# Subtracting the low part of the edge weight unit on GpSimd instead of VectorE in a two-layer DiT kernel

## The reference

```
h = h + 0.5 * mod_l[:, 2] * swiglu(pre_norm(h, norm_g[i, 0], mod_l, 0), ffn_w_in[i, 0], ffn_w_out[i, 0])
hn = pre_norm(h, norm_g[i, 1], mod_l, 1)
h = h + mod_l[:, 5] * y_l
h = h + 0.5 * mod_l[:, 8] * swiglu(pre_norm(h, norm_g[i, 2], mod_l, 2), ffn_w_in[i, 1], ffn_w_out[i, 1])
```

## Time and profile before

| what | us |
|---|---|
| median of 3 runs (lowest, highest) | 3191.51 (3191.02, 3193.46) |
| the profiled execution | 3189.59 |
| its span | 3187.9 |
| PE busy | 3075.0 (96%) |
| DVE busy | 1820.9 (57%) |
| ACT busy | 864.7 (27%) |
| POOL busy | 36.7 (1%) |
| granted TensorE clock, mean | 0.989 |

### The profile page before, as it was taken

How to read it: one execution, slowest core, us unless ns; L and a number is a source line. 1 busy time by engine, 2 the same in 40 slices (tenths; PEclk the granted TensorE clock), 3 DMA queues, 4 the chain that set the end, 5 groups by cost and what they waited for, 6 DMA issues and landing times.

```text
span 3187.9 us, 42477 instructions
## 1 busy us (share of the span) xinstructions
PE 3075.0 (96%) x17592; PEld 2638.7 (83%) x17592; DVE 1820.9 (57%) x2652; ACT 864.7 (27%) x1188; POOL 36.7 (1%) x73
## 2 busy tenths in 40 slices
PE   6999999999999899999999999999899999999999
PEld 4888888877777788888888888888788888888887
DVE  4675565864565576655565365656654546454444
ACT  3211121343443431111223111112322223242221
POOL 0000000000000000000000000000000000000000
PEclk8999999999999999999999999999899999999999
DMA  6332322111010043323221132322111212122222
GB/s 241 133 132 99 112 105 92 53 47 53 27 53 27 30 156 119 119 93 118 105 92 54 66 110 97 112 106 87 53 48 59 79 39 79 40 80 94 97 94 84
DMA packets 40984, 277.81 MB, mean 87 GB/s; under 512 B 4352, under 2 KB 5632, under 8 KB 8000
## 3 DMA queue, kind: packets, MB, share of 16 engines
q1 hardware_dynamic: 31024, 205.85, 17.8%
q0 software_dynamic: 9872, 70.72, 6.2%
HBM read 274.45 MB, written 2.10 MB: 87 GB/s over the span
## 4 chain that ended last, share of the span: by engine, by line
PE 90%; DVE 6%; ACT 2%; issue 1%; DMA 0%; SPq 0%; DVEq 0%; ACTq 0%
PE ps L305 29%; PE ps L306 28%; PE ps L307 28%; PE ps L625 2%; PE ps L333 1%; DVE wl L1273 1%; ACT wh L891 1%; DVE act_buf L1357 1%; DVE xnl L1361 1%; PE ps L319 0%; DMA ada_w<-ada 0%; PE ps L351 0%; ACT xnh L922 0%; DVE nrm L1570 0%; PE ps L418 0%
## 5 line engine op out<-in xcount | busy, mean ns | idle before, releaser
L305 PE MATMUL ps<-xnh,wl 128*128 128x512 f32 (+1 forms) x3040 | 1062.5, 350 | 31.4 <-DVE wl L1273 15.6
L306 PE MATMUL ps<-xnl,wh 128*128 128x512 f32 (+1 forms) x3040 | 1052.3, 346 | 0.0
L307 PE MATMUL ps<-xnh,wh 128*128 128x512 f32 (+1 forms) x3040 | 1051.7, 346 | 0.0
L305 PEld LDWEIGHTS ps<-xnh,wl 128*128 128x128 f32 x3040 | 580.7, 191 | 113.7 <-DVE wl L1273 17.5
L307 PEld LDWEIGHTS ps<-xnh,wh 128*128 128x128 f32 x3040 | 580.9, 191 | 70.8
L306 PEld LDWEIGHTS ps<-xnl,wh 128*128 128x128 f32 x3040 | 581.2, 191 | 68.2 <-issue 1.0
L1273 DVE TENSOR_TENSOR wl<-raw,wh 128x2048 fp32r<-128x2048 f32 (+1 forms) x183 | 410.3, 2242 | 145.3 <-ACT wh L891 145.1
L891 ACT ACTIVATE wh<-raw 128x2048 fp32r<-128x2048 f32 (+1 forms) x178 | 332.7, 1871 | 578.8 <-PE ps L307 578.8
L1415 DVE SCALAR_TENSOR_TENSOR h<-ps,coef,h 128x512 f32<-128x512 f32 x624 | 371.7, 642 | 116.1 <-PE ps L307 115.5
L305 PE MATMUL ps<-hidh,wl 128*128 128x512 f32 (+1 forms) x1232 | 425.0, 345 | 3.1 <-DVE h L1373 3.1
L306 PE MATMUL ps<-hidl,wh 128*128 128x512 f32 (+1 forms) x1232 | 426.0, 346 | 0.0
(11 more groups left out here) (233 smaller groups left out, 3056.9 us busy)
## 6 DMA issues: line engine op xcount, KB each, us to landing
raw<-weights SPq DMA_DIRECT2D x183, 1024.0 KB, 4.8
adaw<-ada POOLq DMA_DIRECT2D x64, 1024.0 KB, 5.0
ada_w<-ada SPq DMA_DIRECT2D x8, 1024.0 KB, 20.0
h<-x_in SPq DMA_DIRECT2D x1, 2048.0 KB, 8.6
c_act<-c_rows POOLq DMA_DIRECT2D x2, 1024.0 KB, 5.1
out<-h SPq DMA_DIRECT2D x8, 256.0 KB, 2.0
h<-x_in SPq DMA_DIRECT2D x1, 1024.0 KB, 28.9
cs<-rope_mla POOLq DMA_DIRECT2D x1, 512.0 KB, 3.5
```

Of the source, the lines that this page charges most:

```text
L305: mm(dst, lhs[1][rows], rhs[0][rows], start=first, stop=False)
L306: mm(dst, lhs[0][rows], rhs[1][rows], start=False, stop=False)
L307: return mm(dst, lhs[0][rows], rhs[0][rows], start=False, stop=last)
```

## The change

The semaphore `edge_hi` is new. ScalarE's last quarter of the edge unit counts it in place of `w_hi[s]`, and `split_lo(s)` goes from VectorE's `last_y`. GpSimd has a new `edge_lo(s)`, which waits for `edge_hi` and does the same subtraction, 128 x 2048, and counts `w_ready[s]`. It is called five times in GpSimd's list: behind the first `ada_loop`, behind the `cs` DMA, behind the 24th unit of the second round (whose loop is cut in two there), and twice at the end.

```diff
+            def edge_lo(s):
+                pool.wait_ge(edge_hi, c.next(edge_hi))
+                nc.gpsimd.tensor_tensor(wl[:, s, :], raw[:, s, :], wh[:, s, :].bitcast(F32), ALU.subtract).then_inc(w_ready[s], 1)
...
             c.next(ada_used, 2)
+            edge_lo(0)
             c.next(xn_ready, 2 * KD)
             pool.wait_ge(xn_ready, c.next(xn_ready, 2 * KD))
             pool.dma_start(cs[:], rope_mla).then_inc(tab_full, 16)
+            edge_lo(1)
             pool.wait_ge(xn_ready, c.next(xn_ready, 2 * KD))
             ada_start(mid)
-            ada_loop(mid + 2, (ADA_UNITS - ADA_0 - mid - 2) // 2)
+            end = ADA_2 - ADA_0
+            ada_loop(mid + 2, (end - mid) // 2)
+            edge_lo(0)
+            ada_loop(end + 2, (ADA_UNITS - ADA_0 - end - 2) // 2)
             pool.wait_ge(ada_used, c.next(ada_used, 2))
             pool.dma_start(cr[:], rope_ret).then_inc(tab_full, 16)
             pool.dma_start(dist[:], dist_in).then_inc(tab_full, 16)
+            edge_lo(1)
+            edge_lo(1)
...
                 if q == 3:
-                    ins.then_inc(w_hi[s], 1)
+                    ins.then_inc(edge_hi, 1)
...
                 add_pair(2 if early is not None else 4, parts[1], banks)
-                split_lo(s)
                 for m in (4, 6) if early is not None else (6,):
```

More of the change, by code:

```diff
@@ L196, in build @@
         ada_full = [sem(f"ada_full{s}") for s in range(2)]
+        edge_hi = sem("edge_hi")
         ada_used, ada_evac = sem("ada_used"), sem("ada_evac")
```

## The result

The changed kernel takes 3212.11 us (median of 4 runs, 3206.92 to 3215.10), the kernel before 3191.9 in the same comparison: a ratio of 1.0062, 95% interval 1.0046 to 1.0077. The forecast was 3211.0. The profiled execution took 3209.45 us with a span of 3207.7, 19.8 more than before.

What follows compares the result with a forecast made beforehand. TensorE, busy for 3075.0 of 3187.9 us, was taken to bound the kernel; 13.1 us of later second chains plus 6.4 of lost clock made 19.5 us slower, a median of 3211.0 us, range 3188 to 3215.

Steps and rivals of the forecast that it cites:

- What can be gained: TensorE's waits for the moved unit at edges 1, 3, 4 and 5: 4.5 us, 0.14% of the time.
- How long GpSimd takes: GpSimd's 128 x 2048 subtraction at each edge: 4.6 us, twice VectorE's time.
- The collision: At the edges, GpSimd's reading may meet VectorE's two-input L1361 rows; taken to delay the second chains by 13.1 us in all.
- The priced end: Each L1361 that falls into GpSimd's 4.6 us waits for its end: 13.1 us over five edges; forecast's chance 0.50.
- the other end: GpSimd and VectorE read beside each other at full pace, no price: sum -2.7 us, 3188.8; chance 0.26.
- Which row: At edge 1 GpSimd gets in behind row 5's low part at 614.60; row 6's low part waits until 619.20.
- The clock: TensorE falls to 1.2 GHz behind the long stalls: 1.6 us at each of edges 1 to 4, 6.4 us.
- By edge: Second chain later by 2.85 us at edges 1, 3 and 4, 2.6 at edge 2, 1.95 at edge 5, before clock loss.
- Shared in turns: GpSimd and VectorE both slowed while overlapping at the edges, none blocked to the end: about +1 us, 3192.5; chance 0.14.
- VectorE wins: GpSimd gets in only behind row 7 at the edges, its unit late: sum 7.3 us, 3198.8; chance 0.07.

Runs made afterwards that it cites:

- the run that only writes: Changed kernel with GpSimd's subtraction replaced by a memset of the same tile to zero: 3183.26 us against 3191.57, ratio 0.9978.
- the plain reordering: Kernel before, with VectorE's whole subtraction moved ahead of the pair of additions, GpSimd not used: 3186.49 us against 3190.94, ratio 0.9985.
- the copy that does: Changed kernel with GpSimd's subtraction replaced by a copy of raw into wl, one SBUF input instead of two: 3189.04 us, ratio 0.9992.
- The filled kernel: Changed kernel with 16 useless matmuls (32 at edge 5) before TensorE's wait for row 5 at each edge: 3204.84 us against 3190.94, ratio 1.0042.
- the run behind row 7: Changed kernel with GpSimd also waiting for the norm's row 7 before it subtracts: 3202.0 us, ratio 1.0037.
- the first quarter: Changed kernel with GpSimd's subtraction cut into four of 512 columns, each behind ScalarE's quarter: 3191.69 us, ratio 1.0002.

## Why the prediction was right

- **What can be gained.** The waits for the moved unit were 4.5 us, and 4.5 us is what went. The squares and additions were early already, and no wait for them came at edges 1 to 4. Right. At edge 5 they are early only while TensorE is slow: with the clock up it waits for the squares, 0.66 us in the run that only writes and 1.42 in the plain reordering.
- **How long GpSimd takes.** 4.52 to 4.55 us, taken as 4.6 from twice VectorE's row. The 4497 ns that the Trainium skill states in "GPSIMD Engine Reference", section 3.1, is 0.02 to 0.05 from it.
- **The collision.** The priced end held: one low part per edge waited for GpSimd's end, shown by the row of 5.07 us, by the write that holds nothing, by the copy that does, and by the additions and squares behind row 7. The traces of before could not tell it from the other end; it was a choice, at a chance of one in two.
- **Which row.** Here the working was off. I had GpSimd come in behind row 5's low part, at 614.60. It started 0.08 us behind ScalarE's last quarter, in the same moment as that low part (614.06 and 614.05), and won; so it did at edges 2 to 4. So TensorE stood with 18 matmuls of the first pass to do instead of 12, and the stall began one row earlier (4.11 us, where I had 3.7). GpSimd also ended 0.6 us earlier for it. At edge 5 it came in behind row 5, as forecast, with the stall at row 6: 3.70 us.
- **The clock.** I had 1.6 us at four edges, 6.4. The filled kernel gives back 2.0, 1.45 and 1.4 at edges 1, 3 and 4. For edge 2 the changed kernel's own timeline has to do: the eight matmuls behind the stall take 3.4 us (1129.20 to 1132.62), and at full clock they would take 1.9, so 1.5. Together 6.4: the sum is right, the distribution not. The 0.9 of edge 5 doesn't belong to it, since the kernel before pays there too, as I had said: its clock is 0.62 behind the wait, and so is the changed kernel's.
- **By edge.** Forecast with the clock 4.45, 4.2, 4.45, 4.45 and 1.95, in all 19.5; measured 5.23, 4.54, 4.70, 4.67 and 1.54, in all 20.7, and 19.8 on the span. Four edges came out 0.2 to 0.8 us longer and the last 0.4 shorter. At edge 2 some 0.5 of it isn't the new stall's: the slow stretch behind the old wait of 4.3 us was that much longer in this execution (the first 15 matmuls take 5.4 us instead of 4.9). That 3211.0 met 3212.1 so closely is luck within a few microseconds; the runs scatter from 3206.9 to 3215.1.
- **The rivals.** "Shared in turns" is excluded by the 5.07 us row. "VectorE wins" was built as the run behind row 7: it cost 10.4 us (12.4 by the edges' lengths) where I had 7.3, since I had left out the clock there. It fell behind the stalls of 2.54 and 2.57 us at edges 3 and 4, not behind the 2.58 at edge 1, and at edge 5 the stall was 3.63 us, with the clock at 0.50 in the next 5.

## What to carry to other kernels

Before work goes from VectorE to GpSimd, look at which VectorE instructions run in the same microseconds and count their SBUF inputs: beside those with two, a GpSimd instruction that reads SBUF isn't parallel work, and what is left of it when they begin is the price. Cut into pieces, such work hides in part, beside VectorE's instructions that read one input from SBUF and one from PSUM. And if an engine waits for one result among several, look first whether it can simply be made earlier in the same queue: one line moved gave 4.5 us here in the medians (3.2 by the edges' lengths), where a second engine cost 20.

## What the runs showed of the hardware

A GpSimd write of 128x2048 (memset, 1.81 us) beside a two-input VectorE instruction holds nothing (0.74 us); a copy of the same size (1.89 us) holds it for 1.67 us. A held VectorE instruction shows no idle time in front: the wait is inside its own duration (5.07 instead of 0.75 us), so it has to be looked for in the longest instruction of a group and not in the list of waits. When both began within 0.01 us of each other, GpSimd went first each time, in eight cases (one piece and the first quarter, at edges 1 to 4). GpSimd's fixed part is small: a quarter took 1.29 us when undisturbed, so four would take 5.2 against 4.52 for one piece, an estimate of 0.2 us for each instruction more. The length of a stall alone didn't tell whether TensorE's clock falls: it was 1.00 behind 1.46 us (one input read) and behind 2.58 (edge 1 of the run behind row 7), but 0.62 behind 1.97 (edge 5 before) and 0.66 behind 2.54 (edge 3 of the run behind row 7). Matmuls whose result is thrown away, issued into a stall of 4.1 us, kept TensorE's clock at 2.4 GHz and gave back up to 2.0 us of work behind it.
